# Sparse-attention heads with the scaling ahead of the turns and a transposed output, bias rows by another path, and stage borders in another order

## The chip, the cores and the metric
One core of one Trainium2 chip runs the whole program. The metric is the device time of one execution in microseconds (us), as the median of several runs; less is better.

## The reference
A sequence of 256 tokens, D = 1024, goes through two blocks. The first: short convolution, squared-ReLU mlp, a gated per-layer embedding (ple), dilated window attention with rotary positions (qkv, wo), a second mlp and ple. The second: two layers, each with a half SwiGLU feed-forward, a mixer and a half feed-forward, where the first mixer is an S5 state-space layer and the second is sparse attention over keys and values computed once, between the layers. Everything is f32 in and out; each stage starts with an RMS norm.
```python
def second_block(...):
    for layer in range(DEPTH):                                   # 2
        h = h + 0.5 * _swiglu(_rmsnorm(h, ffn1_norm), w_in, w_out)   # ffn0, ffn2
        u = _rmsnorm(h, mix_norm[layer])
        h = h + (_s5_mixer(u, ...) if layer < 1 else _nsa_mixer(u, kv, ...))
        h = h + 0.5 * _swiglu(_rmsnorm(h, ffn2_norm), w_in, w_out)   # ffn1, ffn3
        if layer == 0:
            kv = _shared_kv(h, ...)        # 6 x 4 heads of 64; 15 compressed blocks

# _nsa_mixer: 16 query heads on 4 kv heads, head_dim 64
o_cmp = softmax(q @ k_cmp * scale + bias_cmp) @ v_cmp            # 256 x 15
o_slc = softmax(q @ k_slc * scale + bias, causal) @ v_slc        # 256 x 256
o_win = softmax(q @ k_win * scale + bias, causal) @ v_win        # 256 x 256
o = gates[..., 0:1] * o_cmp + gates[..., 1:2] * o_slc + gates[..., 2:3] * o_win
return o @ w_o
```
With 256 tokens the selection (8 blocks of 64) and the window (512) both take in the whole sequence. bias is a relative-position table of 32 buckets, so row t of a head's bias is a piece of one vector of distances, shifted by t.

## The kernel before
The activation h stays in SBUF, transposed (channels in partitions). The weights, 280 units of 128 x 2048 f32 (1 MB each), come by SP's queue into a ring of three slots `raw` (L372 to L397): SP issues the next unit when DVE has finished with its slot (`lo_ready`). ACT copies each unit to `w_hi` (L1024), DVE subtracts to get `w_lo` (L1749, `split`), and PE multiplies in split precision (`double_unit` L453 and L455, `exact` L407 to L409). The order of the work on each engine is written out by hand, with semaphores between the engines; nothing is scheduled by a compiler. Zero matmuls (`keep_warm` L510, L513) fill some of PE's pauses.

**A stage border.** A norm is: ACT squares (L1048), POOL adds them (L1545), PE sums over the channels (`norm_sum` L515), DVE takes the variance (L1766), POOL the power (L1553), DVE forms a diagonal (L1770), PE spreads it to all channels (`norm_bcast` L524, L526), ACT copies it to `rs`. DVE's part is `norm(n)` (L1764). In `mlp` (L1831) and `ffn` (L1869) DVE runs it behind `whole(0)` (L1826, a sum of two PSUM banks, recorded at L1828) and `split(g)`. In `ple` (PE L622, DVE L1927) four gate units are multiplied into two banks, so PE waits for DVE's `gate_scaled` ahead of the third and fourth. Behind the first ple DVE computes the rotary angles in eight steps (L2032 to L2040), waits for ACT's sines (`sin_ready`), and only then runs the norm for qkv.

**The tables of S5.** POOL builds eight tables of the state-space kernel in `make_table` (L1611), four of them beside each mlp, in a chain that waits for its own stores; PE takes one at positions `TABLE_AT` (L156) of the mlp's units in `table_turn` (L539, L548) and waits for `tab_ready` (L1634) there.

**The bias rows.** In ffn1 ACT issues, one for each pair of units, `side_loads` (L1134): a store of two heads of the bias vector, each 128 times, to DRAM (L1138, `bias_rows`, 16 x 128 x 383 floats in all), and a load of a piece of `cmp_w1` (L1141). ACT waits for all stores ahead of ffn2, and in ffn2 it loads the rows back (`load_rows` L1144, L1150) into `tbl` with a stride of 382, so that each partition gets its shifted row.

**The heads.** Sixteen heads, one step each (L1008 to L1018 on PE). PE: `n_turn(h)` waits for the exps, turns (transposes) six tiles of 128 x 128 and two of 15 columns (L966, L969) behind 8 zero matmuls (16 for the first); `n_scores(h+1)` (L938) multiplies q with the two key sets and the compressed keys, `n_values(h)` (L972, L985 to L993) multiplies the turned probabilities, stationary, with the values, 64 columns each; every second head `n_turn_out` (L997, L1004) turns the combined output back, behind 6 zero matmuls. ACT: `n_copy` (L1489) copies the first branch and the compressed part out of PSUM, `n_exp` (L1497, L1501 to L1506) takes the exps with their sums, `n_high` (L1510) the high half of the output. DVE: `window_copy` (L2323, L2327) copies the second branch, `logits` (L2303, L2309 to L2320) scales, adds the bias and takes the maxima, `combine` (L2329) forms gate / denominator (L2333, L2336) and scales and sums the three outputs (L2348, L2350), `n_low` (L2353) gives the low half. POOL does nothing in the heads.

## Time and profile before
| | |
|---|---|
| runs shown, median (lowest to highest) | 2113.27 us (2112.58 to 2115.02), 3 runs |
| the profiled execution | 2118.91 us, its span 2116.7 us |
| PE / DVE / ACT / POOL busy | 1976.0 (93%) / 1326.1 (63%) / 934.8 (44%) / 581.7 (27%) us |
| chain that ended last | PE 66%, DVE 12%, ACT 6%, POOL 6%, issue 5%, ACT's queue 3% |
| mean granted clock of PE | 0.967 |
| zero matmuls (L513) in the whole span | 356 recorded in the page's group, 95.1 us |
| weight units | 280 of 1024 KB, 4.8 us from issue to landing (median) |

The profile shows one execution. Busy time of an engine is the time its instructions ran; PE's clock is what the throttle granted, 1.00 being 2.4 GHz and 0.50 being 1.2 GHz. "Idle before, releaser" is how long an engine stood still ahead of an instruction, and what it waited for; "issue" is idle time in which it waited for nothing that the profile shows. The chain that ended last is followed back from the last instruction, at each step to what released it.

### The profile page before, as it was taken

The page shows a single profiled execution, that of the slowest core. Times are in us where ns is not written, and L with a number is a line of the kernel's source. Part 1 is how long each engine was busy: PE and PEld are TensorE (multiplying, and loading weights), DVE is VectorE, ACT ScalarE, POOL GpSimd, SP SyncE. Part 2 cuts the span into 40 slices and gives each one's busy share as a digit, 9 for nine tenths or more (in the row PEclk, how much of TensorE's full clock was granted, in tenths as well). Part 3 has the DMA queues.
Part 4 walks back from the last instruction along what each step waited for, and adds up shares of the span by engine and source line. Part 5 has one row for each costly group of instructions (what it writes and reads, how often), then busy time and mean ns, then how long its engine had stood idle before and what let it go on. Part 6 is the DMA issues. An engine that isn't in the chain of part 4 may idle for free.

```text
span 2116.7 us, 32243 instructions
## 1 busy us (share of the span) xinstructions
PE 1976.0 (93%) x13621; PEld 1779.6 (84%) x13655; DVE 1326.1 (63%) x1653; ACT 934.8 (44%) x1196; POOL 581.7 (27%) x692
## 2 busy tenths in 40 slices
PE   8989998999988998989998999878999989999999
PEld 7979997899987998959997888778799976667998
DVE  6877666566556676666667565456466665546665
ACT  4344454444444444444442353245544453434443
POOL 6967831543223978410005300000000000000000
PEclk9999999999999999999999899999999989999999
DMA  6446663443432455565545156454255520004552
GB/s 240 179 159 219 215 223 123 174 150 140 148 132 112 187 214 194 189 241 187 188 179 184 56 181 227 162 188 160 106 198 196 192 110 21 1 1 159 181 189 108
DMA packets 54939, 339.48 MB, mean 160 GB/s; under 512 B 5995, under 2 KB 13196, under 8 KB 17932
## 3 DMA queue, kind: packets, MB, share of 16 engines
q1 hardware_dynamic: 41552, 295.41, 38.1%
q10 hardware_dynamic: 9276, 27.34, 3.7%
q0 software_dynamic: 3968, 14.68, 2.0%
q8 instruction: 108, 1.77, 0.3%
q14 instruction: 35, 0.29, 0.0%
HBM read 318.54 MB, written 18.87 MB: 159 GB/s over the span
## 4 chain that ended last, share of the span: by engine, by line
PE 66%; DVE 12%; ACT 6%; POOL 6%; issue 5%; ACTq 3%; DMA 1%; POOLq 0%; DVEq 0%
PE psum L453 17%; PE psum L407 10%; PE psum L409 10%; PE psum L408 10%; PE psum L455 9%; DVE w_lo L1749 4%; ACT w_hi L1024 3%; ACTq L1141 2%; PE psum L513 2%; DVE both L1756 1%; POOL pw L1625 1%; ACT both L1024 1%; POOL pw L1624 1%; DVE h L1762 1%; POOL st L1626 1%
## 5 line engine op out<-in xcount | busy, mean ns | idle before, releaser
L1749 DVE TENSOR_TENSOR w_lo<-raw,w_hi 128x2048 fp32r<-128x2048 f32 x277 | 649.7, 2349 | 249.2 <-ACT w_hi L1024 246.3
L453 PE MATMUL psum<-both,w_hi 128*128 128x512 f32 x2112 | 759.3, 402 | 8.1 <-DVE both L1756 4.3
L1024 ACT ACTIVATE w_hi<-raw 128x2048 fp32r<-128x2048 f32 x280 | 533.1, 1907 | 151.1 <-PE psum L409 142.3
L455 PE MATMUL psum<-both,w_lo 128*128 128x256 f32 x2112 | 596.4, 282 | 0.0
L453 PEld LDWEIGHTS psum<-both,w_hi 128*128 128x128 f32 x2112 | 401.2, 190 | 107.2 <-DVE both L1756 6.4
L407 PE MATMUL psum<-both,w_hi 128*128 128x256 f32 x1472 | 432.6, 294 | 37.1 <-DVE w_lo L1749 22.6
L408 PE MATMUL psum<-both,w_hi 128*128 128x256 f32 x1472 | 423.1, 287 | 0.0
L409 PE MATMUL psum<-both,w_lo 128*128 128x256 f32 x1472 | 422.6, 287 | 0.0
L455 PEld LDWEIGHTS psum<-both,w_lo 128*128 128x128 f32 x2112 | 403.3, 191 | 0.3
L407 PEld LDWEIGHTS psum<-both,w_hi 128*128 128x128 f32 x1472 | 288.8, 196 | 37.3 <-DVE w_lo L1749 18.7
L1545 POOL TENSOR_TENSOR ssum<-sq 128x512 f32<-128x512 f32 x13 | 20.2, 1557 | 1016.1 <-ACT sq L1048 956.4
L408 PEld LDWEIGHTS psum<-both,w_hi 128*128 128x128 f32 x1472 | 289.1, 196 | 2.0 <-issue 1.4
L409 PEld LDWEIGHTS psum<-both,w_lo 128*128 128x128 f32 x1472 | 288.5, 196 | 0.0
L1024 ACT ACTIVATE sq<-psum 128x512 f32<-128x512 f32 x120 | 71.5, 596 | 310.5 <-PE psum L455 310.4
L407 PE MATMUL psum<-hid_hi,w_hi 128*128 128x256 f32 x640 | 184.4, 288 | 4.2 <-DVE w_lo L1749 3.3
L408 PE MATMUL psum<-hid_lo,w_hi 128*128 128x256 f32 x640 | 181.9, 284 | 0.0
L409 PE MATMUL psum<-hid_hi,w_lo 128*128 128x256 f32 x640 | 181.8, 284 | 0.0
L407 PEld LDWEIGHTS psum<-hid_hi,w_hi 128*128 128x128 f32 x640 | 123.5, 193 | 8.0 <-DVE w_lo L1749 4.6
L408 PEld LDWEIGHTS psum<-hid_lo,w_hi 128*128 128x128 f32 x640 | 123.5, 193 | 0.1
L409 PEld LDWEIGHTS psum<-hid_hi,w_lo 128*128 128x128 f32 x640 | 123.5, 193 | 0.0
L1828 DVE TENSOR_TENSOR ta<-psum,sq 128x512 f32<-128x512 f32 x76 | 52.3, 688 | 108.9 <-ACT sq L1024 108.9
L513 PE MATMUL psum<-zero 128*128 128x512 bf16 x356 | 95.1, 417 | 12.6 <-DVE both L2355 7.2
(349 smaller groups left out, 2569.4 us busy)
## 6 DMA issues: line engine op xcount, KB each, us to landing
raw<-in_weights SPq DMA_DIRECT2D x280, 1024.0 KB, 4.8
table<-tables ACTq DMA_DIRECT2D x8, 1792.0 KB, 8.5
tables<-st POOLq DMA_DIRECT2D x16, 512.0 KB, 4.6
tables<-st POOLq DMA_DIRECT2D x8, 384.0 KB, 4.4
bias_rows<-bv ACTq DMA_DIRECT2D x8, 383.0 KB
tables<-st POOLq DMA_DIRECT2D x8, 256.0 KB, 7.4
w<-in_cmp_w ACTq DMA_DIRECT2D x4, 512.0 KB, 27.4
tbl<-in_cmp_w ACTq DMA_DIRECT2D x4, 512.0 KB, 30.8
```

The costliest lines, as they stand in the source:

```text
L407: nc.tensor.matmul(out, a_hi, b_hi, start=start, stop=False, skip_group_check=True)
L408: nc.tensor.matmul(out, a_hi, b_lo, start=False, stop=False, skip_group_check=True)
L409: return nc.tensor.matmul(out, a_lo, b_hi, start=False, stop=stop, skip_group_check=True)
L453: nc.tensor.matmul(bank, wh[:, cols], both[x][:, c].rearrange("p e t -> p (e t)"), start=c == 0, stop=False, skip_group_check=True)
L455: return nc.tensor.matmul(bank[:, 0:SEQ], wl[:, cols], x_hi[x][:, c], start=False, stop=c == KC - 1, skip_group_check=True)
L513: nc.tensor.matmul(bank, zero[:, 0:P], zero[:], start=True, stop=True, skip_group_check=True)
L1024: copy = lambda out, in_, **kw: nc.scalar.activation(out, in_, ACT.Copy, **kw)
L1141: act.dma_start([w1[:], w1v][k // 4][:, at], A["cmp_w1"][k // 4][:, at])\
L1624: tt(pw[:, 0], old, a_re, ALU.mult)
L1625: link(tt(pw[:, 1], old, a_im, ALU.mult))
L1749: tt(w_lo[:, g % RING], raw[:, g % RING], w_hi[:, g % RING].bitcast(F32), ALU.subtract).then_inc(sem["lo_ready"], 1)
L1828: tt(ta[:], hi_part(pair), low[into], ALU.add).then_inc(sem["a_sum"], 1)
```

## The change
**Heads.** The softmax factor (gate / denominator) is now multiplied into the probabilities ahead of the turns: the first branch on DVE (`scale`), the second branch and the compressed part on POOL. The values are now the stationary side and the turned probabilities the moving one, all three branches are summed in one PSUM region of 64 x 256, already transposed, so the combine and the turn of the output go. The logits of both branches are written by wide operations over two neighbouring banks. ACT makes all copies. All zero matmuls in the heads go. PE's order in a step is values of two heads back, scores of the next, turn of the last.
**Bias rows.** One store of the bias vector (16 x 383); 128 row loads of one partition each on SP, four behind each of 32 weight loads from ffn2's fourth unit on.
**Borders.** DVE's norm goes ahead of `whole(0)` and `split(g)` in `mlp` and `ffn`; ple's gate units go to four places in three banks; the rotary angles go into the first ple's loop and the norm ahead of the wait for the sines; three of the table positions of the second mlp move by one.
```diff
-TABLE_AT = ((1, 4, 8, 12), (2, 6, 10, 14))
+TABLE_AT = ((1, 4, 8, 12), (3, 7, 11, 14))
...
+    bias_v = A["bias_v"].tensor
+    def bias_row(p):
+        row = bass.AP(bias_v, P - 1 - p, [[NH * NDIST, 1], [NDIST, NH], [1, SEQ]])
+        sp.dma_start(tbl[p:p + 1], row).then_inc(sem["tbl_landed"], 16)
...
             sp.wait_ge(sem["lo_ready"], RING * k + (u + 1 - RING))
             sp.dma_start(raw[:, u:u + 1], A["weights"][bass.ds(RING * k + u, 1)]
                          .rearrange("o p n -> p o n")).then_inc(raw_landed[u], 16)
+            at = RING * k + u - BASE["ffn2"] - RING
+            if at == 0:
+                sp.wait_ge(sem["bias_stored"], 16)
+                sp.wait_ge(sem["hid_done"], 4)
+            if 0 <= at < 32:
+                for p in range(4 * at, 4 * at + 4):
+                    bias_row(p)
...
+    GB = [DB[3], U[0], U[1], DB[3]]
...
         for m in range(PAIRS):
-            if m >= 2:
-                pe.wait_ge(sem["gate_scaled"], PAIRS * l + m - 1)
-            up_unit(g + 1 + m, 0, XBUF[n], U[m % 2], (sem["xl_ready"], XBASE[n], 1) if m == 0 else None,
+            if m == 3:
+                pe.wait_ge(sem["gate_scaled"], PAIRS * l + 1)
+            up_unit(g + 1 + m, 0, XBUF[n], GB[m], (sem["xl_ready"], XBASE[n], 1) if m == 0 else None,
                     (lambda: norm_sum(n)) if m == 0 else (lambda: norm_bcast(n)) if m == 1 else None)
         pe.wait_ge(sem["gate_scaled"], PAIRS * (l + 1) - 1)
...
         for br in range(2):
-            bank = DB[2 * br + b]
+            bank = DB[2 * b + br]
...
     def n_turn(hd):
         b = hd % 2
-        if hd >= 2:
-            pe.wait_ge(sem["n_lo"], hd // 2)
         if hd:
-            pe.wait_ge(sem["n_tv"], hd)
             pe.wait_ge(sem["n_ta"], hd)
-        keep_warm(8 if hd else 16, U[0])
-        pe.wait_ge(sem["n_exp"], hd + 1)
+        pe.wait_ge(sem["n_near"], hd + 1)
+        pe.wait_ge(sem["n_far"], hd + 1)
         for br in range(2):
             for j in range(3):
-                last = nc.tensor.transpose(U[br][:, j * P:(j + 1) * P], lg[:, b, br, j * P:(j + 1) * P],
-                                           ident)
-        for t in range(TT):
-            last = nc.tensor.transpose(MB[0:NCMP, t * P:(t + 1) * P], lgc[:, b, t, :], ident)
+                nc.tensor.transpose(U[br][:, j * P:(j + 1) * P], lg[:, b, br, j * P:(j + 1) * P], ident)
+            last = nc.tensor.transpose(U[br][0:NCMP, 3 * P:4 * P], lgc[:, b, br, :], ident)
         last.then_inc(sem["n_t"], 1)
     def n_values(hd):
-        b, kh = hd % 2, 2 * (hd // 8) + hd % 2
-        if hd:
-            pe.wait_ge(sem["n_part"], 3 * hd)
-        pe.wait_ge(sem["n_tv"], hd + 1)
+        b, kh, ch = hd % 2, 2 * (hd // 8) + hd % 2, hd // 2
+        out = [XB, MB][ch % 2][b * HD:(b + 1) * HD, 0:SEQ]
+        if b == 0 and ch >= 2:
+            pe.wait_ge(sem["n_lo"], ch - 1)
         pe.wait_ge(sem["n_ta"], hd + 1)
         dims = slice(kh * HD, (kh + 1) * HD)
-        def out(br, t):
-            at = (br * TT + t) * HD
-            return XB[:, at:at + HD]
-        for t in range(TT):
-            nc.tensor.matmul(out(0, t), ptc[:, b, t * P:(t + 1) * P], vcmp[:, kh, :], start=True, stop=True,
+        nc.tensor.matmul(out, vcmp[:, kh, :], ptc[:, b, :], start=True, stop=False, skip_group_check=True)
+        for br in range(2):
+            nc.tensor.matmul(out, vs[:, br, 0, dims], ptn[:, b, br, 0:SEQ], start=False, stop=False,
                              skip_group_check=True)
-        for br in range(2):
-            pb_ = ptn[:, b, br]
-            nc.tensor.matmul(out(1 + br, 0), pb_[:, 0:P], vs[:, br, 0, dims], start=True, stop=True,
-                             skip_group_check=True)
-            nc.tensor.matmul(out(1 + br, 1), pb_[:, P:2 * P], vs[:, br, 0, dims], start=True, stop=False,
-                             skip_group_check=True)
-            last = nc.tensor.matmul(out(1 + br, 1), pb_[:, 2 * P:3 * P], vs[:, br, 1, dims], start=False,
-                                    stop=True, skip_group_check=True)
+            last = nc.tensor.matmul(out[:, P:SEQ], vs[:, br, 1, dims], ptn[:, b, br, SEQ:SEQ + P], start=False,
+                                    stop=br == 1, skip_group_check=True)
         last.then_inc(sem["n_pv"], 1)
-    def n_turn_out(ch):
-        keep_warm(6, U[0])
-        pe.wait_ge(sem["n_part"], 6 * ch + 6)
-        if ch:
-            pe.wait_ge(sem["n_lo"], ch)
-        for t in range(TT):
-            last = nc.tensor.transpose(MB[:, SEQ + t * P:SEQ + (t + 1) * P],
-                                       oc[:, ch % 2, t].rearrange("p e d -> p (e d)"), ident)
-        last.then_inc(sem["n_ot"], 1)
     n_scores(0)
-    for step in range(NH + 1):
-        if step:
-            n_turn(step - 1)
+    for step in range(NH + 2):
+        if step >= 2:
+            n_values(step - 2)
         if step + 1 < NH:
             n_scores(step + 1)
-        if step:
-            n_values(step - 1)
-        if step and step % 2 == 0:
-            n_turn_out(step // 2 - 1)
+        if 1 <= step <= NH:
+            n_turn(step - 1)
     residual_units("nwo", 0, (sem["n_lo"], 0, 2))
...
         act.wait_ge(sem["bv_copied"], 1)
+        act.dma_start(A["bias_v"], bv[:]).then_inc(sem["bias_stored"], 16)
     def side_loads(k):
         if 0 <= k < PIECES:
-            heads = slice(NH // PIECES * k, NH // PIECES * (k + 1))
-            act.dma_start(A["bias_rows"][heads], bv[heads].unsqueeze(1)
-                          .broadcast_to([NH // PIECES, P, NDIST])).then_inc(sem["bias_stored"], 16)
             at = slice(CL // 4 * (k % 4), CL // 4 * (k % 4 + 1))
             act.dma_start([w1[:], w1v][k // 4][:, at], A["cmp_w1"][k // 4][:, at])\
                 .then_inc(sem["cmpw_landed"], 16)
-    def load_rows(k):
-        if k < PIECES:
-            at = NH // PIECES * k
-            rows_ = bass.AP(A["bias_rows"].tensor, P - 1 + at * P * NDIST,
-                            [[NDIST - 1, P], [P * NDIST, NH // PIECES], [1, SEQ]])
-            act.dma_start(tbl[:, at:at + NH // PIECES], rows_).then_inc(sem["tbl_landed"], 16)
...
-            if f == 2:
-                load_rows(k)
...
-    act.wait_ge(sem["bias_stored"], 16 * PIECES)
...
-        copy(ptn[:, b, 0], U[0][:, 0:3 * P])
-        copy(ptc[:, b], MB[0:NCMP, 0:SEQ]).then_inc(sem["n_ta"], 1)
+        for br in range(2):
+            copy(ptn[:, b, br], U[br][:, 0:3 * P])
+            last = copy(ptc[:, b, br * P:(br + 1) * P], U[br][0:NCMP, 3 * P:4 * P])
+        last.then_inc(sem["n_ta"], 1)
...
+    for hd in range(NH):
+        b = hd % 2
+        pool.wait_ge(sem["n_fac"], hd + 1)
+        for t in range(TT):
+            pool.tensor_scalar(lgc[:, b, t], lgc[:, b, t], fac[:, b, 0, t:t + 1], None, ALU.mult)
+        pool.tensor_scalar(lg[:, b, 1, 0:P], lg[:, b, 1, 0:P], fac[:, b, 2, 0:1], None, ALU.mult)
+        pool.tensor_scalar(lg[:, b, 1, P:3 * P], lg[:, b, 1, P:3 * P], fac[:, b, 2, 1:2], None,
+                           ALU.mult).then_inc(sem["n_far"], 1)
...
         split(late)
+        norm(n)
         whole(0, hb)
         split(g)
-        norm(n)
         dve.wait_ge(sem["rs_ready"], n + 1)
...
         if late is not None:
             split(late)
+        if n is not None:
+            norm(n)
         whole(0, hb)
         split(g)
         if n is not None:
-            norm(n)
             dve.wait_ge(sem["rs_ready"], n + 1)
...
+    def angles(m):
...
-            tt(ta[:], two(U[m % 2]), rs_b, ALU.mult).then_inc(sem["gate_scaled"], 1)
+            tt(ta[:], two([DB[3], U[0], U[1], DB[3]][m]), rs_b, ALU.mult).then_inc(sem["gate_scaled"], 1)
             gated(PAIRS * l + m + 1, two([XB, DB[0], DB[1], DB[2]][m]), m)
             if x:
                 x_low(r, m)
             if m < 2:
                 split(g + 1 + m)
+            if l == 0:
+                angles(m)
...
+    norm(R_PLE0)
     dve.wait_ge(sem["sin_ready"], 3)
-    norm(R_PLE0)
...
-        stt(lgc[:, b].rearrange("p t c -> p (t c)"), DB[b][:, 3 * P:3 * P + TT * NCMP], NSCALE,
+        stt(lgc[:, b].rearrange("p t c -> p (t c)"), DB[2 * b][:, 3 * P:3 * P + TT * NCMP], NSCALE,
             cmp_bias[:, :, hd], ALU.mult, ALU.add)
-        for br in range(2):
-            bank = DB[2 * br + b]
-            stt(lg[:, b, br, 0:P], bank[:, 0:P], NSCALE, near, ALU.mult, ALU.add)
-            last = stt(lg[:, b, br, P:3 * P], bank[:, P:3 * P], NSCALE, far, ALU.mult, ALU.add)
-        last.then_inc(sem["n_log"], 1)
+        banks = psum[:, 2 * b:2 * b + 2]
+        stt(lg[:, b, :, 0:P], banks[:, :, 0:P], NSCALE, near.unsqueeze(1).broadcast_to([P, 2, P]),
+            ALU.mult, ALU.add)
+        stt(lg[:, b, :, P:3 * P], banks[:, :, P:3 * P], NSCALE, far.unsqueeze(1).broadcast_to([P, 2, SEQ]),
+            ALU.mult, ALU.add).then_inc(sem["n_log"], 1)
         dve.wait_ge(sem["n_log"], hd + 1)
         dve.tensor_reduce(nm[:, b, 0, :], lgc[:, b], AX.X, ALU.max, negate=True)
-        for br in range(2):
-            dve.tensor_reduce(nm[:, b, 1 + br, 0:1], lg[:, b, br, 0:P], AX.X, ALU.max, negate=True)
-            last = dve.tensor_reduce(nm[:, b, 1 + br, 1:2], lg[:, b, br, P:3 * P], AX.X, ALU.max, negate=True)
-        last.then_inc(sem["n_max"], 1)
-    def window_copy(hd):
-        dve.wait_ge(sem["n_t"], hd + 1)
-        if hd >= 2:
-            dve.wait_ge(sem["n_pv"], hd - 1)
-        dve.tensor_copy(ptn[:, hd % 2, 1], U[1][:, 0:3 * P]).then_inc(sem["n_tv"], 1)
-    def combine(hd):
+        dve.tensor_reduce(nmx[:, b], lg[:, b].rearrange("p r (j k) -> p r j k", j=3), AX.X, ALU.max,
+                          negate=True).then_inc(sem["n_top"], 1)
+        dve.wait_ge(sem["n_top"], hd + 1)
+        tt(nm[:, b, 1:3, 1], nmx[:, b, :, 1], nmx[:, b, :, 2], ALU.min).then_inc(sem["n_max"], 1)
+    def scale(hd):
         b = hd % 2
         dve.wait_ge(sem["n_exp"], hd + 1)
@@ -2335,35 +2324,24 @@
         dve.wait_ge(sem["n_rec"], hd + 1)
         tt(fac[:, b], fac[:, b], gate[:].rearrange("p t (r n) -> p r t n", n=NH)[:, :, :, hd],
            ALU.mult).then_inc(sem["n_fac"], 1)
-        dve.wait_ge(sem["n_pv"], hd + 1)
         dve.wait_ge(sem["n_fac"], hd + 1)
-        for br in range(3):
-            if br:
-                dve.wait_ge(sem["n_part"], 3 * hd + br)
-            for t in range(TT):
-                at = (br * TT + t) * HD
-                out = oc[:, hd // 2 % 2, t, b]
-                f = fac[:, b, br, t:t + 1]
-                if br:
-                    last = stt(out, XB[:, at:at + HD], f, out, ALU.mult, ALU.add)
-                else:
-                    last = ts(out, XB[:, at:at + HD], f, None, ALU.mult)
-            last.then_inc(sem["n_part"], 1)
+        ts(lg[:, b, 0, 0:P], lg[:, b, 0, 0:P], fac[:, b, 1, 0:1], None, ALU.mult)
+        ts(lg[:, b, 0, P:3 * P], lg[:, b, 0, P:3 * P], fac[:, b, 1, 1:2], None,
+           ALU.mult).then_inc(sem["n_near"], 1)
     def n_low(ch):
         dve.wait_ge(sem["n_hi"], ch + 1)
-        tt(x_lo[0][:, ch], MB[:, SEQ:2 * SEQ], x_hi[0][:, ch].bitcast(F32),
+        tt(x_lo[0][:, ch], [XB, MB][ch % 2][:, 0:SEQ], x_hi[0][:, ch].bitcast(F32),
            ALU.subtract).then_inc(sem["n_lo"], 1)
-    for step in range(NH + 1):
-        if step:
-            window_copy(step - 1)
+    for step in range(NH + 2):
         if step < NH:
             logits(step)
-        if step:
-            combine(step - 1)
-        if step and step % 2 == 0:
-            n_low(step // 2 - 1)
+        if 1 <= step <= NH:
+            scale(step - 1)
+        if step >= 5 and step % 2:
+            n_low((step - 5) // 2)
+    n_low(NQ - 1)
     residual_stage("nwo", R_NWO)
     ffn(3, R_NWO, R_FFN3, x=False, late=BASE["nwo"] + 3)
```

## Rows read from the trace of the kernel before
**Rows 1.** Busy time by stretch: PE, PEld, DVE, ACT, POOL, PE clock, DMA share, GB/s
```profile
1755.85:1894.45 138.60, 126.14 (x763) 91.65 (x777) 77.36 (x311) 53.64 (x231) 0.00 (x0) 0.95 0.00 1
1234.01:1449.15 215.14, 189.82 (x1208) 172.83 (x1209) 120.00 (x106) 85.95 (x85) 4.06 (x3) 0.94 0.55 186
1522.51:1705.76 183.25, 180.92 (x1205) 165.24 (x1206) 120.92 (x106) 87.45 (x86) 4.04 (x3) 1.00 0.52 191
130.30:137.10 6.80, 5.23 (x15) 4.44 (x16) 3.32 (x5) 1.92 (x4) 6.34 (x10) 0.50 0.61 248
935.80:939.20 3.40, 3.40 (x12) 2.90 (x11) 0.69 (x1) 2.57 (x4) 0.00 (x0) 0.50 0.98 418
```
**Rows 2.** Groups of instructions in the heads (busy, mean ns, idle before)
```profile
L513 PE MATMUL psum<-zero 128*128 128x512 bf16 x170 | 45.5, 408 | 8.2 <-DVE both L2355 7.2 <-issue 0.6
```
**Rows 3.** Timeline of PE in one head (start, duration, line)
```profile
1812.98 0.82 PE L966 MATMUL psum<-con,lg 128*128 128x128 f32 x6
...
1813.94 0.48 PE L944 MATMUL psum<-ks,q 64*128 64x128 f32 x2
...
1814.27 0.59 PE L946 MATMUL psum<-ks,q 64*128 64x256 f32 x2
...
1814.70 0.38 PE L944 MATMUL psum<-ks,q 64*128 64x128 f32 x2
...
1815.80 0.65 PE L985 MATMUL psum<-vcmp,ptc 15*128 15x64 f32 x4
```
**Rows 4.** Timeline of ACT in the same head
```profile
1814.05 0.49 ACT L1024 ACTIVATE ptn<-psum 128x384 f32<-128x384 f32 x1 [3.33 <-PE psum L969]
...
1814.44 0.36 ACT L1024 ACTIVATE ptc<-psum 15x256 f32<-15x256 f32 x1
```
**Rows 5.** Timeline of DVE in the same head
```profile
1814.53 0.19 DVE L2309 SCALAR_TENSOR_TENSOR lgc<-psum,cmp_bias 128x30 f32<-128x30 f32 x1
...
1816.95 0.18 DVE L2333 RECIPROCAL fac<-dn 128x6 f32<-128x6 f32 x1
```
**Rows 6.** POOL's scalings, lines L1647 and L1581 (duration min/median/max)
```profile
L1647 POOL TENSOR_SCALAR st<-st x8: 858/863/1063, 103.5 to 858.4; 128x256 f32<-128x256 f32 x8
...
L1581 POOL TENSOR_SCALAR sm<-a x1: 312/312/312, 29.9 to 29.9; 128x32 f32<-128x32 f32 x1
```
**Rows 7.** Timeline of PE: norm_bcast at mlp0, qkv, ffn0 and ffn3
```profile
131.87 1.22 PE L526 MATMUL psum<-diag,ones 128*128 128x256 f32 x2 [3.56 <-DVE diag L1770]
...
375.66 1.22 PE L526 MATMUL psum<-diag,ones 128*128 128x256 f32 x2 [6.19 <-DVE diag L1770]
...
935.20 0.70 PE L526 MATMUL psum<-diag,ones 128*128 128x256 f32 x2 [2.58 <-DVE diag L1770]
...
1931.13 0.70 PE L526 MATMUL psum<-diag,ones 128*128 128x256 f32 x2 [3.34 <-DVE diag L1770]
```
**Rows 8.** Timeline of DVE: the angles, and ffn3's start
```profile
368.36 0.29 DVE L2033 CAST ang<-posi 128x256 f32<-128x256 int32 x1
...
371.11 0.29 DVE L2040 TENSOR_SCALAR ang<-ang 128x256 f32<-128x256 f32 x1
...
1926.76 0.68 DVE L1828 TENSOR_TENSOR ta<-psum,sq 128x512 f32<-128x512 f32 x1
...
1929.69 0.15 DVE L1766 TENSOR_SCALAR var_tok<-psum 128x2 f32<-128x2 f32 x1
```
**Rows 9.** Timeline of PE and POOL: table turns and the fourth table in mlp1
```profile
799.72 1.54 PE L548 MATMUL psum<-con,ab 128*128 128x128 f32 x6 [6.16 <-POOL st L1634]
...
845.25 0.20 POOL L1634 COPY st<-e 128x8 f32<-128x8 f32 x1
...
848.25 1.04 PE L548 MATMUL psum<-con,ab 128*128 128x128 f32 x8
```
**Rows 10.** DMA issues on ACT and SP by line (time held, min/median/max)
```profile
L1141 ACTq DMA_DIRECT2D tbl<-in_cmp_w x4: 6352/15442/19212, 1338.0 to 1399.3; - x4
...
L388 SPq DMA_DIRECT2D raw<-in_weights x276: 327/328/328, 18.1 to 2077.9; - x138
```

60 lines of the change are left out of this document (32 added, 28 removed).

## The prediction

> **What bounds the kernel now.** I read the engines' shares first: PE is busy 93% of the span and carries 66% of the chain that ended last, so time goes only where PE idles, runs zero products, or runs at the lower clock. The table by stretch [rows 1] shows where that is. In the heads PE is "busy" 126.1 of 138.6 us, but 45.5 us of that are zero matmuls [rows 2]; POOL does nothing there, DVE and ACT are busy about half. ffn1 needs 215.1 us for its body, ffn2 183.3 for the same products, with PE busy 189.8 and 180.9: that is a stall. The last two stretches show PE at half clock (0.50, the 1.2 GHz level) behind a pause at a stage border. Then I read, engine by engine, one step of the heads [rows 3 to 5] and the borders [rows 7 to 9]. The sum is made against the profiled execution, 2118.9 us; the median of the runs shown is 5.6 lower, which I take off at the end. A measurement of this kernel can tell about 0.2% (4.2 us).
>
> **Heads.** Before, 138.6 / 16 = 8.66 us a head: one chain (turn, copies, products, combine) whose gaps the zero matmuls fill. The 184 zero matmuls go, yet what they cover is waiting, so their 45.5 us are not the gain; the new period is. PE's loop is now turn(h), a wait for its copies, values(h), scores(h+3), turn(h+1). In one head [rows 3]: turn 1812.98 to 1813.94 = 0.96; scores 1813.94 to 1815.80 = 1.86; a product over 256 columns 0.43 (1814.27 to 1814.70), so new values, three of 256 and two of 128 columns, 3x0.43 + 2x0.22 = 1.73. ACT now copies both banks: 2x0.39 (starts 1814.05 and 1814.44) plus two 15-partition pieces, bounded by 0.36 for 256 columns [rows 4], taken 0.2 each, plus drain: 1.27. PE's loop if nothing else bounds: 0.96 + 0.1 + 1.27 + 0.1 + 1.73 + 1.86 = **6.0**.
> The other loop goes through DVE and POOL. DVE's logits(h+2) wait for turn(h) and stand in its queue ahead of the factor of h+1; POOL's scaling of h+1 waits for that factor, and turn(h+1) for the scaling; the exps lie beside it. Serial: turn 0.96 + 0.1; logits and maxima, 1814.53 to 1816.95 = 2.42 (now wider but the same columns; the reduces cover 768 at once); reciprocal 0.18 [rows 5] and a product of its size, 0.39 with what lies between; POOL's scalings of 15, 15, 128 and 256 columns. No row shows POOL scaling with a per-partition pointer. The nearest are 0.86 for 128x256 and 0.31 for 128x32 [rows 6], so 0.27, 0.27, 0.55, 0.86 = 1.95, taken 2.2 with a little for each pointer; bounds 1.8 and 3.2. With it, 0.96 + 0.1 + 2.42 + 0.39 + 2.2 + 0.1 = **6.2** a head. ACT's share, 53.6 / 16 = 3.35 [rows 1] plus the copy taken over, and DVE's, 77.4 / 16 = 4.8 less the combine, stay under it. So POOL's loop just binds: 10.7 until the pipeline is full, 15 x 6.2, 3.1 behind the last: about 106. With the zeros gone PE is idle some 4 us ahead of the first turn and some 2 us a head later; I add 3 for the start and 5 for stretches at half clock (before, even with zeros, 0.95 [rows 1]). 114 against 138.6: **-25**, between -33 (POOL 1.8, no clock loss) and -18 (POOL at 2.7, 6.7 a head: 8 us more).
> POOL and DVE now both scale at the same time. No row shows such a pair. The Trainium skill, "SBUF — State Buffer", "Who interferes with whom", says that a tensor_scalar in DVE's two-port mode and a GpSimd operation lock each other out wholly; by it each head would lose up to 0.5, DVE's two scalings at no more than the 0.29 of a scaling of 256 columns [rows 8], and the total would come out near 2042.
>
> **Bias rows, the ACT queue in ffn1.** Eight stores of two heads x 128 copies x 383 floats become one of 16 x 383. Before, the eight loads of cmp_w1 queued behind these stores held ACT, the last four 6.4 to 19.2 us each [rows 10], so its copies of the weights, and PE with them, came late. With short queues ffn1 should run as ffn2 does: 215.14 - 183.25 = **-31.9** [rows 1]. Ends: 0 (the loads of cmp_w1 hold ACT by themselves) to -32. I take the whole: the hold grows from piece to piece (loads of equal size, 6.4 at the least, 19.2 at the most), as it would behind stores that pile up, and not if it were the load's own cost.
> **Row loads on SP.** 128 small DMAs, four behind each of 32 weight loads. An issue on SP takes 0.33 us [rows 10], so four take 1.3 of the 5.7 us that a unit lasts (183.25 over some 32 units); the DMA share in ffn2 is 0.52 [rows 1], and 128 rows of 16 KB put 2 MB beside its 32. The wait on the bias store lies far behind it, and the wait on the compressed hidden states is met before ffn2's first split. ACT loses eight issues. **0**, hidden by the slack of a ring of three; bounds -1 and the rival below.
>
> **Norm ahead of whole and split.** At each border PE waits for DVE's diag [rows 7]: 3.56 (mlp0), 2.58 (ffn0), 3.34 (ffn3). In ffn3 DVE does whole and split from 1926.76 to 1929.69 first [rows 8]: 2.9 us that now follow the norm. What is late next is the first relu or SwiGLU product, which needs the broadcast anyway, and the split of the next unit, 2 units ahead. mlp0: wait 3.56 to about 0.3, -3.2; behind it PE runs at half clock with 5.23 busy in 6.8 [rows 1], full clock would save 2.6: **-5.8**. ffn0: -2.6 and half of the 3.4 at 0.50 [rows 1]: **-4.3**. ffn3 likewise: **-4.4**. ffn1's small wait is left at 0. The clock part is the choice here; without it the three give 6 us less.
> **qkv's start.** PE waits 6.19 for diag [rows 7]; DVE does the angles from 368.36 to 371.40, 3.0 us [rows 8], then waits for ACT's sines until the norm. The norm no longer waits for them: -3.3 and a part of the clock. But six of the eight steps, 2.3 of the 3.0, now lie ahead of ple0's last x_low, which the same norm needs; the rope waits later then end sooner. **-4** of a possible -6.
> **mlp1 and the tables.** The norm saves 3 here too, but POOL's tables bound this stage: PE waits 6.16 for one at 799.72, and the fourth is ready only at 845.25, turned at 848.25 [rows 9]. POOL starts 2.9 earlier, so the fourth is there at about 842.3. Positions 3, 7, 11 for 2, 6, 10 put the turns later where they waited; the fourth position is unchanged, so PE arrives there early and the stall goes to the last table. End of the stage: 848.25 to 842.3, -5.9, less 2.4 of half clock behind a wait of some 10 us: **-3.5**.
> **ple.** Gates in other banks take two PE waits away, but DVE's and ACT's gate work sets that stage: **0** (bounds -2, +1).
> Sum: 25 + 31.9 + 5.8 + 4.3 + 4.4 + 4 + 3.5 = 78.9. 2118.9 - 78.9 = 2040.0; less 5.6: **2034**.
>
> **Rivals.**
> (a) PE's clock. The zeros held the clock; without them PE idles 2 of 6.2 us a head, and if the chip grants 1.2 GHz throughout, PE's part 4.55 doubles: 10.7 a head, 174 us for the heads, 60 more: 2094. For: the half-clock stretches [rows 1] follow pauses of 3 us. Against: a pause here is 2 us or less, and turns recur. 0.12, mostly in milder forms of 2040 to 2075.
> (b) POOL at 1.8 and no clock loss: PE's loop binds, 6.0 a head, about 2023. 0.17.
> (c) The change does not do what it says in ffn1: the hold is cmp_w1's own, 512 KB a load with pieces of its own; none of the last four was issued in less than 6.4 us [rows 10]. Then 31.9 stays: 2066. 0.12.
> (d) Slower. The row loads do on SP what the stores did on ACT. A store had 256 pieces (2 heads x 128) and held the issue behind it up to 19.2 us [rows 10], 0.075 a piece. Four rows are 64 pieces, 4.8 us a unit, in series with a weight load's 4.8 (the profile's section of DMA issues): 9.6 against 5.7 a unit, 3.9 x 32 = 125 more: 2159. It decides from 79 / 32 = 2.5 us a unit, or 0.053 a piece: 3.4 us a unit, of which 5.7 - 4.8 = 0.9 is slack. Against: the 0.52 share of DMA in ffn2 leaves room. 0.05.
> The store's access pattern has an outermost dimension of 2 heads, a row load's of 16. By the Trainium skill, "DMA: Bandwidth & Descriptors", "Why a DMA increments its semaphore by 16 and not by 1", the engines used are the largest number up to 16 that divides that dimension: two for the store, 16 for a row. By that rule the long hold of 19.2 us is the store's and (c) and (d) both fall away.
> **How the numbers follow.** Forecast 0.54, (a) 0.12, (b) 0.17, (c) 0.12, (d) 0.05. The range goes from (b) with a little more (2014) to beyond (c) (2074); it leaves out (d), the full form of (a) and a sum with two misses. Faster in all but (d) and the worst of (a) with (c): 0.93; within 0.2%: 0.01; slower: 0.06.
>
> **What would show it.** Heads: 6.0 to 6.4 us between turns, POOL busy about 2.2 a head, n_turn waiting for POOL rather than ACT; granted clock 0.9 or more. ffn1's body 183, no ACT issue over 3 us. ffn2's body 183 still. Diag waits under 1 us. In mlp1 one long wait at the fourth table near 832. Wrong if the heads' clock reads 0.5, if ffn1 stays above 200, or if ffn2 grows.

## The result, and the profile after

The changed kernel takes 2083.35 us (median of 4 runs, 2074.79 to 2089.9) where the kernel before takes 2114.14; the ratio is 0.985, interval 0.9803 to 0.9896. It is 1.5% faster, by 31 us where 79 were forecast, and lies outside the range of 2014 to 2074. Its runs are 15 us apart, those of before 5. One execution of one experiment (e9), the profiled one, took 2330.6 us at a mean clock of 0.746; its time and its trace are left out below. The profiled execution took 2088.89 us, 30.0 less than the one of before.

The page of the changed kernel: engines, PE's clock in 40 slices, and the chain that ended last.
```profile
PE 1966.1 (94%) x13339; PEld 1768.8 (85%) x13359; DVE 1301.9 (62%) x1509; ACT 941.0 (45%) x1228; POOL 619.9 (30%) x756
...
PEclk9999999999999999999998999999999975569999
...
PE 69%; DVE 11%; POOL 9%; ACT 7%; issue 3%; DMA 1%; ACTq 0%; POOLq 0%; DVEq 0%
```
Four slices stand out at 7, 5, 5 and 6 tenths: they are the heads. ACT's queue, 3% of the chain before, is gone from it.

The table by stretch of the changed kernel, which answers to [rows 1]: the heads, the bodies of ffn1 and ffn2, and the end of mlp1 from the fourth table's turn to the next broadcast.
```profile
core 0: us, PE busy (x) PEld busy (x) DVE busy (x) ACT busy (x) POOL busy (x), PEclk, DMA share, GB/s
1707.40:1868.70 161.30, 137.97 (x480) 96.42 (x480) 54.11 (x170) 59.52 (x263) 35.68 (x64) 0.55 0.00 1
1218.97:1402.70 183.73, 181.40 (x1207) 165.82 (x1208) 121.02 (x106) 86.93 (x85) 4.04 (x3) 1.00 0.54 201
1474.60:1658.19 183.59, 181.27 (x1206) 165.66 (x1206) 121.01 (x106) 87.49 (x86) 4.04 (x3) 1.00 0.55 190
834.01:874.78 40.77, 38.85 (x296) 38.33 (x298) 23.44 (x37) 14.98 (x19) 17.03 (x37) 0.88 0.46 168
```
The heads grew from 138.6 to 161.3 us, with the clock at 0.55 for 0.95. PE has 480 records there for 763, yet was busy 138.0 us for 126.1. ffn1's body fell from 215.14 to 183.73, just ffn2's. The last stretch took 36.47 us before, at full clock:
```profile
848.25:884.72 36.47, 34.54 (x298) 34.02 (x298) 28.02 (x40) 17.79 (x22) 19.11 (x35) 1.00 0.68 243
```

One step of the heads on PE, timeline of the changed kernel (start, duration), with the pause between turn and values:
```profile
1780.30 0.90 PE L978 MATMUL psum<-con,lg 128*128 128x128 f32 x3
...
1783.61 1.08 PE L990 MATMUL psum<-ptc,vcmp 15*64 15x256 f32 x2 [1.34 <-ACT ptc L1012]
...
1787.37 0.79 PE L959 MATMUL psum<-ks,q 64*128 64x128 f32 x2
...
1790.90 0.90 PE L978 MATMUL psum<-con,lg 128*128 128x128 f32 x3
```
A step is 1780.30 to 1790.90 = 10.6 us: turn and copies 3.3, values and the issue behind them 3.8, scores 3.5. These are the terms of the forecast with each of PE's about doubled; the copies alone kept their 1.3. Of the fifteen steps between turns nine take 10.5 to 10.6 us at a clock of 0.50, four 9.5 to 9.7 at 0.56 to 0.62, and the last two 7.3 and 4.9. The waits of PE in the heads say what bounds:
```profile
PE psum L990 <- ACT ptc L1012: 20.6, 16, 1.3
PE psum L978 <- POOL lg L1715: 2.7, 2, 2.5
```
PE waits 16 times for the copies and only twice for POOL. POOL's scalings, of which no row was at hand, came as estimated, 1795.78 to 1798.00 = 2.22 us for 2.2 (x2 stands for two instructions merged in one line):
```profile
1795.78 0.75 POOL L1713 TENSOR_SCALAR lgc<-lgc,fac 128x15 f32<-128x15 f32 x2 [8.37 <-DVE fac L2325]
...
1796.50 0.60 POOL L1714 TENSOR_SCALAR lg<-lg,fac 128x128 f32<-128x128 f32 x1
...
1797.08 0.92 POOL L1715 TENSOR_SCALAR lg<-lg,fac 128x256 f32<-128x256 f32 x1
```

The borders, which answer to [rows 7]: the broadcasts of mlp0, qkv and ffn3 on PE.
```profile
128.71 0.70 PE L541 MATMUL psum<-diag,ones 128*128 128x256 f32 x2 [0.67 <-DVE diag L1755]
...
366.48 0.70 PE L541 MATMUL psum<-diag,ones 128*128 128x256 f32 x2 [0.38 <-DVE diag L1755]
...
1902.69 0.70 PE L541 MATMUL psum<-diag,ones 128*128 128x256 f32 x2 [0.43 <-DVE diag L1755]
```
Waits of 3.56, 6.19 and 3.34 became 0.67, 0.38 and 0.43. DMA issues that touch `tbl`, which answer to [rows 10] (ns held, min/median/max):
```profile
L388 SPq DMA_DIRECT2D tbl<-bias_v x128: 481/589/2236, 1457.8 to 1633.8; - x128
...
L1127 ACTq DMA_DIRECT2D tbl<-in_cmp_w x4: 334/334/335, 1314.2 to 1365.4; - x4
```
The loads of cmp_w1 that held ACT for 6.4 to 19.2 us hold it for 0.33. A row load costs SP 0.59.

From broadcast to broadcast (the stages' first broadcasts in both traces), forecast against measured, in us:

| stage | forecast | measured |
|---|---|---|
| mlp0 and ple0 | -5.8 | -7.1 |
| qkv, with its part of the clock in attention | -4 | -4.1 (40.87 to 38.78, and 298.32 to 293.31 less mlp1's earlier norm, 3.0) |
| mlp1 | -3.5 | +1.3 (3.0 earlier, then 210.74 to 215.00) |
| ffn0 | -4.3 | -4.4 (19.73 to 16.98, 190.92 to 189.24) |
| ffn1 with its start | -31.9 | -32.1 |
| kv, ffn2, qg | 0 | -1.1 |
| heads | -25 | +22.6 (138.7 to 161.3) |
| nwo, ffn3 | -4.4 | -4.9 |

Two rows failed: the heads by 47.6 and mlp1 by 4.8. All others together were forecast within 4 us.

### The profile page after: what moved, and what is told of

Read it like the earlier page. It is cut to its first block, busy times and chain, and to the rows that moved or that the text cites. A ratio compares the mean times of both kernels' runs of the same rounds, so it can differ in the third digit from the quotient of the medians.

```text
span 2086.8 us, 31686 instructions
## 1 busy us (share of the span) xinstructions
PE 1966.1 (94%) x13339; PEld 1768.8 (85%) x13359; DVE 1301.9 (62%) x1509; ACT 941.0 (45%) x1228; POOL 619.9 (30%) x756
## 4 chain that ended last, share of the span: by engine, by line
PE 69%; DVE 11%; POOL 9%; ACT 7%; issue 3%; DMA 1%; ACTq 0%; POOLq 0%; DVEq 0%
PE psum L468 19%; PE psum L421 10%; PE psum L423 10%; PE psum L422 10%; PE psum L470 10%; DVE w_lo L1734 4%; ACT w_hi L1012 3%; DVE both L1741 2%; POOL pw L1602 1%; PE psum L992 1%; POOL pw L1601 1%; PE psum L961 1%; PE psum L978 1%; POOL st L1603 1%; ACT both L1012 1%
## 5 line engine op out<-in xcount | busy, mean ns | idle before, releaser
L1662 POOL TENSOR_TENSOR swap<-swap,sin_rs 32x512 f32<-32x512 f32 x24 | 44.6, 1859 | 122.7 <-DVE swap L2082 122.7
```

The source lines that it names most:

```text
L1662: pool.tensor_tensor(swap[:], swap[:], sin_rs[0:32].unsqueeze(1).broadcast_to([32, 2, SEQ]), ALU.mult).then_inc(sem["sin_part"], 1)
```

## The experiments

Times are medians, with the ratio to the kernel before, run on the same chip beside it. Those kernels before took 2114 to 2117 us, so between two experiments the ratios compare better than the times. "Heads" is the time from the first scores to the last values, "step" the time between two turns. Five theories meet in the heads: the clock fell in the pause ahead of the first turn; the pause between turn and values keeps it down; the share of time in which PE is busy does; the kind of work (turns, products on 64 rows) does; or the clock only follows, and a new loop of turn, copies and values bounds the step (the "dependency theory").

**e1, the heads of before in the changed kernel.** Edit: PE, ACT, DVE and POOL heads put back, of which on PE:
```diff
-                pe.wait_ge(sem["n_near"], hd + 1)
-                pe.wait_ge(sem["n_far"], hd + 1)
+                keep_warm(8 if hd else 16, U[0])
+                pe.wait_ge(sem["n_exp"], hd + 1)
...
+                if step and step % 2 == 0:
+                    n_turn_out(step // 2 - 1)
```


> The changed kernel with the heads of before (their zero matmuls and combine too); all else of the change stays. Between before and after the stages other than the heads lose 52.5 us by the traces and the heads gain 22.6. If the parts add up: heads 138.7 us, time 2114 - 52.5 = 2061 to 2062, and it beats the changed kernel by some 20. If a part of the gain elsewhere came only together with the new heads, it is above 2065.

Measured 2068.8 us, ratio 0.9783 (0.976 to 0.9806), heads 138.3. The rest of the change is worth 48 us by the kernel before beside it (2116.5) for the 52.5 of the sum; the new heads cost 14 of it by the medians. The time lies above the 2065 that was to mean that a part of the gain came only with the new heads. The trace doesn't bear that out: ahead of the heads it is 3.2 us behind the changed kernel's, mainly 1.6 by the first broadcast, 1.6 in mlp0 (200.6 for 199.0) and 1.3 in ffn2's stretch, and the first two differences stand also between kernels that have the same code there (in mlp0 e2 took 200.4, e5 199.1).

**e2, scores ahead of values.**
```diff
-                if step >= 2:
-                    n_values(step - 2)
                 if step + 1 < NH:
                     n_scores(step + 1)
+                if step >= 2:
+                    n_values(step - 2)
```


> In a step PE's scores go ahead of the values, so that ACT's copies of a turn run beside the scores and not in an idle PE (1.3 us a head). Clock theory (PE's idle time lets the clock fall, and at 1.2 GHz PE's own work sets the step of 10.6): the step is PE's work alone at half clock, 10.6 - 1.3 - 0.5 = 8.8 to 9, heads 145 or less (less where the busier engine gets full clock at times), time 2060 to 2068. Dependency theory (the new loop turn, copies, values bounds, and the clock only follows): the step falls to 6.2 to 7 at once, time below 2040. Kind-of-work theory (turns and products of 64 rows do not hold the clock however dense they are): granted clock stays 0.5, heads 145, 2068.

Measured 2046.6 us (2045.0 to 2049.2), ratio 0.9674 (0.9652 to 0.9695), heads 114.9. The first step took 9.2 at half clock; then the clock rose and stayed for eleven steps. Behind them it fell twice more, for 6.8 us each time, and came back (steps of 7.4, 7.0 and 6.2). One full step and a stretch of eight, timeline and table by stretch of e2:
```profile
1758.81 0.52 PE L978 MATMUL psum<-con,lg 128*128 128x128 f32 x3 [1.43 <-POOL lg L1715]
...
1759.80 0.48 PE L959 MATMUL psum<-ks,q 64*128 64x128 f32 x2
...
1761.66 0.64 PE L990 MATMUL psum<-ptc,vcmp 15*64 15x256 f32 x2
...
1765.17 0.52 PE L978 MATMUL psum<-con,lg 128*128 128x128 f32 x3 [1.43 <-POOL lg L1715]
```
```profile
1745.00:1796.00 51.00, 39.46 (x240) 29.21 (x240) 26.73 (x84) 30.07 (x134) 18.04 (x34) 1.00 0.00 1
```
The step is 6.36 us and PE waits for POOL ahead of the turn, both as forecast (6.2). The theory of the kind of work falls: the same turns and products run at 1.00. No total of the three was met: the step is that of the dependency theory (6.2 to 7), the 2046.6 is not (below 2040).

**e3, eight zero matmuls of 256 columns in the pause.**
```diff
+                for _ in range(8):
+                    nc.tensor.matmul([XB, MB][ch % 2][:, SEQ:2 * SEQ], zero[:, 0:P], zero[:, 0:SEQ],
+                                     start=True, stop=True, skip_group_check=True)
                 pe.wait_ge(sem["n_ta"], hd + 1)
```


> Eight zero matmuls of 256 columns (0.85 us at full clock) in the pause between a turn and the values, into unused columns of the output's bank. Clock theory by idle share: PE is busy 5.4 of 6.2 us again, as dense as before the change (126 of 138.6), granted clock 0.9 or more, step 6.2 to 6.5, heads 105 to 115, time 2030 to 2042. Dependency theory or kind-of-work theory: at half clock the zeros take 1.7 us where 1.3 were idle, step 11, time about 2090.

Measured 2042.8 us, ratio 0.9656 (0.9636 to 0.9677), heads 108.3, step 6.36 in the changed kernel's own order:
```profile
1737.40:1800.00 62.60, 57.87 (x375) 43.59 (x376) 33.43 (x105) 36.72 (x162) 21.53 (x40) 1.00 0.01 1
```
Putting 128 zero matmuls of half the width back gains 40 us over the changed kernel. The dependency theory falls here, since the order is unchanged and the step is 6.36, not 11. Heads met what was expected, the total misses it by 1.

**e4, scores first and 8 wide zero matmuls ahead of each turn** (`keep_warm(8 if hd else 16, U[0])` behind the wait on `n_ta`).

> Scores ahead of the values, and 8 zero matmuls of 512 columns (1.7 us at full clock) ahead of each turn's wait for the scalings, 16 ahead of the first. Clock theory: PE is busy nearly always, clock 0.95 or more, step max(6.2, 4.55 + 1.7 + 0.2) = 6.45, heads 103 to 112, time 2028 to 2040. If the clock stays at 0.5 whatever fills the pauses: step 9 + 3.4 = 12.4, heads 200, time 2120.

Measured 2043.0 us, ratio 0.9659 (0.9637 to 0.9681), clock 1.00 from the first turn on, step 6.58: the zeros just overrun the wait they fill. Heads 112.0, at the upper end of what was expected; the total misses it by 3.

**e5, a full clock at the start only** (`keep_warm(28, U[0])` for head 0, none later).

> 28 zero matmuls ahead of the first turn alone, none later: the heads begin at full clock. Start theory (the clock fell in the pause ahead of the first turn, and the step at half clock, with its pause between turn and values, never earns it back): it stays near 1.0, step 6.4 as in the two kernels with full clock, heads 108 to 116, time 2040 to 2048. Pause theory (the step of the changed kernel loses the clock by itself, wherever it begins): it falls within a few steps, step 9.5 to 10.6, heads 150 to 165, time 2078 to 2090.

Measured 2077.8 us (2071.2 to 2088.7), ratio 0.9825 (0.9785 to 0.9866). The table by stretch of e5, five steps before and five after the fall:
```profile
1731.10:1762.80 31.70, 24.95 (x151) 18.22 (x151) 16.52 (x52) 18.56 (x82) 11.14 (x20) 1.00 0.00 1
1772.50:1825.30 52.80, 46.35 (x152) 32.26 (x151) 16.87 (x53) 18.55 (x82) 11.14 (x20) 0.50 0.00 1
```
The same work takes 31.7 us and then 52.8. The start theory falls: the order runs at full clock for six steps of 6.35 and loses it in the seventh. It then stays at half clock for 68 us, till the last steps, though PE is busy 88% there and 79% before. That is the pause theory's course, but later than "within a few steps": heads 143.6 in this trace, for 150 to 165. The runs' times go with their mean clocks (0.962 at 2071.2, 0.950 at 2088.7; in the changed kernel 0.956 at 2074.8, 0.947 at 2089.9), so the spread is probably how long the heads stay at half clock; only one execution of each was profiled, so this is not shown.

**e6, e3's zeros on 64 rows** (`zero[0:64, 0:P], zero[0:64, 0:SEQ]`).

> The eight zero matmuls of 256 columns in the pause, but over 64 rows of the array instead of 128. If all columns count alike: as with 128 rows, step 6.36, 2039 to 2045. If rows count: half clock, step 11, 2090.

Measured 2045.9 us (2 runs), ratio 0.9669 (0.9644 to 0.9695), heads 118.6, 10 more than e3: two steps at half clock (11.0 and 10.0), then 6.36. Once the clock is up, 64 rows hold it. The return was slow: PE ran the first 19.8 us behind the first turn at half clock without a pause, where e3 ran 3.0.
```profile
1719.65:1739.44 19.79, 19.79 (x68) 12.98 (x69) 6.35 (x20) 7.22 (x32) 4.47 (x8) 0.50 0.00 1
```
Whether that is the rows or chance, one trace doesn't tell.

**e7, turns in the pause** (eight `nc.tensor.transpose(..., ident, ident)` for e3's zeros).

> Eight f32 transposes of the identity (128 columns each, 0.9 us at full clock) in the same pause instead of zero matmuls. If turns keep the clock as products do: step 6.4, 2040 to 2046. If turns do not count: the clock stays 0.5 and they add 1.9 us where 1.3 were idle, step 11.2, time 2090 to 2100.

Measured 2037.0 us (2 runs), ratio 0.9627 (0.9601 to 0.9654), heads 112.5, full clock from the second step on. The Trainium skill, "TensorE: Matmul & The Clock Gate", "Part 4: PE-mode transpose", says that turns don't count as PE being busy in the same way. Here f32 turns in the pause held the clock at 1.00 as well as zero matmuls did; in this trace the rule doesn't decide.

**e8, the loop shortened.** e2, 3 zero matmuls ahead of each turn, and the far branch's 256 columns scaled by DVE:
```diff
-                pool.tensor_scalar(lg[:, b, 1, P:3 * P], lg[:, b, 1, P:3 * P], fac[:, b, 2, 1:2], None,
-                                   ALU.mult).then_inc(sem["n_far"], 1)
...
+                ts(lg[:, b, 1, P:3 * P], lg[:, b, 1, P:3 * P], fac[:, b, 2, 1:2], None,
+                   ALU.mult).then_inc(sem["n_near"], 1)
```


> Scores ahead of values, 3 zero matmuls of 512 columns ahead of each turn (16 ahead of the first), and the 256-column scaling of the far branch moved from POOL to DVE. If the loop turn, logits, factor, scaling bounds the step at full clock as the forecast says, it loses POOL's 0.92 and becomes 5.4 to 5.5, heads 96 to 99, time 2024 to 2030. If DVE's three scalings and POOL's two hold each other up, POOL's 128 columns take over 0.6 each and the step stays at 5.9 or more, 2034.

Measured 2030.9 us, ratio 0.96 (0.9581 to 0.9618), step 5.50 as expected; heads 100.4 and the time lie about 1 above what was expected. Timeline of e8, POOL and DVE, and twelve steps in its table by stretch:
```profile
1761.16 0.86 POOL L1714 TENSOR_SCALAR lgc<-lgc,fac 128x15 f32<-128x15 f32 x2 [4.18 <-DVE fac L2325]
...
1761.59 0.39 DVE L2330 TENSOR_SCALAR lg<-lg,fac 128x256 f32<-128x256 f32 x1
...
1761.87 0.60 POOL L1715 TENSOR_SCALAR lg<-lg,fac 128x128 f32<-128x128 f32 x1
```
```profile
1729.70:1795.70 66.00, 65.05 (x392) 47.12 (x398) 43.45 (x137) 44.89 (x200) 15.79 (x36) 1.00 0.00 1
```
The step lost 0.86 of POOL's 0.92, so the loop of the forecast did bound it, as PE's wait of 1.43 for POOL in e2 says too. Now PE is busy 65.05 of 66.00 us and waits for no engine: its own work with the three zero matmuls bounds. POOL's first two scalings grew from 0.75 to 0.86 beside a third one of DVE, the 0.60 did not grow. Of the 0.5 a head that the rule of the Trainium skill, "SBUF — State Buffer", "Who interferes with whom" (named in the prediction), put at risk, 0.1 shows in this step; in the changed kernel the first scaling of 15 columns, beside DVE's two, took 0.56 and the second 0.34, so that some 0.1 may be lost there already (an estimate from these two).

**e9, the old table positions on e8.**

> On the fastest kernel so far (e8: scores ahead of values, three zero matmuls, far branch's 256 columns on DVE), the table positions of before, 2, 6, 10, 14 for 3, 7, 11, 14. Theory: POOL's chain sets mlp1, and the later positions only gathered PE's waits into one of 11.5 us at the fourth table, behind which PE runs 4.3 us longer than before the change; with the old positions the wait is split over the third and fourth, the stage from broadcast to broadcast falls from 214.95 to 211 to 212, time 2027 to 2028. Rival: the later positions are what keeps the stage at 215, then the old ones give 217 or more and 2033.

Measured 2032.3 us (3 runs, 2030.6 to 2034.0), ratio 0.9599 (0.9581 to 0.9617), where e8 has 0.96. The 3 to 4 us less of the theory do not show. The total is within 1 of the rival's 2033, but its 2 us over e8 are less than the interval, and no trace shows the stage: by the times alone the positions are worth nothing that can be told.

**e10, the old bias path on e8** (stores and row loads on ACT back, SP's out).

> e8 with the bias rows by the old path (eight stores and eight loads on ACT, no row loads on SP). If the whole 31.9 us of ffn1 are the stores': ffn1 to kv 224.6 for 193.3, time 2030.9 + 31.5 = 2062. If cmp_w1's loads held ACT in part: less than 31 more. If the row loads on SP cost anything in ffn2, ffn2's stretch falls by it.

Measured 2053.0 us, ratio 0.9697 (0.9681 to 0.9712), 22 more than e8. ffn1's body in e8 and in e10:
```profile
1221.15:1405.07 183.92, 181.60 (x1207) 165.79 (x1208) 121.03 (x106) 86.97 (x85) 4.04 (x3) 1.00 0.56 200
```
```profile
1215.89:1427.03 211.14, 192.08 (x1209) 174.94 (x1208) 120.05 (x106) 86.02 (x85) 4.04 (x3) 0.94 0.57 190
```
The path costs 27.2 us in its stage, 4 less than expected, and the total is 9 below the 2062 that was expected. The issues of the eight loads of cmp_w1 held ACT for 92.2 us together in e10, 95.4 in the kernel before and 2.7 in the changed one: the hold comes with the stores, and it was 3 us shorter here. ffn2's stretch is 255.3 for 255.5, so that the row loads on SP cost nothing that can be seen. The total moved 5 less than the stage; in the two traces the S5 mixer, between ffn0 and ffn1, was 2.4 shorter in e10, and other stages by less.

**e11, DVE's norm behind whole and split again, on e8.**

> e8 with DVE's norm behind whole and split again in both mlps and all ffns. Forecast: mlp0 +5.8, ffn0 +4.3, ffn1 +1, ffn3 +4.2, time some 14 to 15 more but for mlp1. In mlp1 theory A (a split that runs beside POOL's table chain holds POOL up by about 2 us each; with the norm first two more splits fall into it) gives POOL the chain of before, 172.7 from its power to the fourth table for 175.4 to 178, so that mlp1 ends no later than now: total 2043 to 2045. Theory B (the chain's length is chance, and the norm first is a gain there too): mlp1 3 more, 2047 to 2049, chain 175 or more.

Measured 2042.0 us, ratio 0.9639 (0.962 to 0.966), 11 more than e8. By stages mlp0 +3.2, ffn0 +2.8 and +1.6, ffn3 +4.3, attention and mlp1 together +4.6, and, where nothing was edited, the S5 mixer -3.8 and the heads -5.2, which happened to begin at full clock. POOL's chain to the fourth table took 178.1, not 172.7: theory A's number is missed. Its first part shows: the first table came 28.6 us behind POOL's power with four splits in that time, 31.0 with five. The rest can't be told from chance: with one and the same code in this stage the chain took from 175.4 (the changed kernel, e8) to 178.1 us (e2).

**e12 and e14, zero matmuls in the wait for the fourth table.** e12 on e8; e14 takes 60 and, ahead of the first turn of the heads, 8 for 16:
```diff
+                if c == 7:
+                    keep_warm(44, MB)
                 pe.wait_ge(sem["tab_ready"], c + 1)
```


> e8 with 44 zero matmuls of 512 columns (9.4 us at full clock) in PE's wait of 11.5 us for the fourth table of mlp1. If what the stage lost behind that wait is the clock (40.8 us from the fourth turn to the next broadcast for 36.5 before the change): 4 us less, stage 211, time 2026 to 2027. If it is something else: 2031 as before, or 1 to 3 more where the zeros are late.

> e12 with 60 zero matmuls for 44 in the wait for the fourth table, and 8 for 16 ahead of the first turn of the heads (where 16 at half clock take 6.8 us and delay it). If the clock behind the fourth table is what the stage lost and e12's zeros were only too few for its wait (3.8 us stayed idle): 36.5 us from the turn to the next broadcast for 40.5, stage 212 to 214; heads up to 4 less; time 2020 to 2026. If neither: 2031.

Measured: e12 2025.75 us (2019.1 to 2032.4), ratio 0.9568 (0.9539 to 0.9597); e14 2025.6 (2023.9 to 2026.8), ratio 0.9583 (0.9554 to 0.9613). From the fourth turn to the next broadcast, e12 and e14:
```profile
837.84:878.30 40.46, 38.56 (x298) 37.94 (x298) 23.62 (x37) 15.01 (x19) 17.10 (x37) 0.89 0.46 170
```
```profile
835.60:872.07 36.47, 34.55 (x297) 34.02 (x297) 24.68 (x37) 14.99 (x19) 16.74 (x36) 1.00 0.52 188
```
In e12 the fourth table came later, 3.8 us stayed idle behind the zeros, and nothing was won in this stretch; that its total met the expectation is due to heads of 95.2 us, which happened to begin at full clock. In e14 the wait was filled: clock 1.00 and 36.47, to the hundredth what it was before the change. What mlp1 lost behind its long wait is the clock. The fewer zeros at the heads' start brought nothing (heads 100.0 for 100.4).

**e13, more work with the pause left as it is** (the changed order, 8 wide zero matmuls ahead of each turn).

> The changed kernel's order with 8 zero matmuls of 512 columns (1.7 us at full clock) ahead of each turn's wait, 16 ahead of the first; the pause of 1.3 us between a turn and its values stays as it is. Share theory (what counts is the share of time in which PE works): at full clock PE would be busy 4.6 + 1.7 of 7.7 us a step, 81%, more than the 72% of e2, which kept the clock; then full clock, step 7.6 to 7.8, heads 130 to 138, time 2056 to 2066. Pause theory (the pause between turn and values, which a lower clock doesn't shorten, keeps the clock from coming back once it is lost): half clock for most of the heads, step up to 13.7, heads 170 to 215, time 2095 or more.

Measured 2063.9 us, ratio 0.9766 (0.973 to 0.9802), heads 131.1, as the share theory expected (its step was to be 0.1 shorter):
```profile
1736.60:1800.00 63.40, 52.47 (x302) 35.47 (x305) 26.71 (x84) 29.90 (x132) 17.83 (x32) 1.00 0.00 1
```
Clock 1.00, step 7.93, PE busy 83%, and the pause of 1.3 us is still there: the pause alone does not bring the clock down. That it keeps a lost clock from coming back is not tested by e13, whose clock was up before the first turn and never fell. The share alone does not decide the fall either: at 77% (39.46 of 51.00) e2 lost the clock after eleven steps, at 79% (24.95 of 31.70) e5 after six. The two differ in the return. Table by stretch at half clock, of the changed kernel, then of e2:
```profile
1741.22:1799.25 58.03, 51.48 (x164) 35.43 (x165) 19.00 (x61) 21.31 (x96) 13.38 (x24) 0.50 0.00 0
```
```profile
1724.00:1733.58 9.58, 9.58 (x32) 6.81 (x33) 3.17 (x10) 3.61 (x16) 2.24 (x4) 0.50 0.00 0
```
```profile
1805.26:1812.09 6.83, 6.83 (x25) 4.67 (x24) 2.39 (x8) 3.02 (x15) 2.24 (x4) 0.50 0.00 0
```
With a pause of 1.3 us in each step PE stood at half clock for 58 us at a time (68 in e5); without one, busy for the whole stretch, the clock was back within 10 us in e2, within 9 in e7 and within 20 in e6 (e2's last fall, with one pause in it, lasted 6.8 too). So the traces agree with the pause theory for the return, but no run changes the pause alone at half clock; the changed kernel's clock did rise twice for 3.4 us in spite of it; and what makes it fall stays open.

## Why the prediction was wrong

- **The term that failed is the clock in the heads.** The forecast took 5 us for "stretches at half clock" from the 0.95 of before. With the clock held the heads take 108.3 us (e3), in the changed kernel 161.3 at 0.55: the term measured 53. The forecast gave the full form a small part of rival (a)'s 0.12, because "a pause here is 2 us or less". Rival (a) was the outcome: its price, PE's 4.55 doubled and 10.7 a head, was met (10.6), and its 2094 is within 11 us of the measured time (its heads of 174 are 13 too long, since the clock rose at times); only its chance was too low. The argument against it was wrong twice: pauses of 1.3 us did not let the clock stay (e5), and the 0.95 of before was the clock with the zero matmuls in it, which the change takes away. An operation whose only purpose is to be work for PE can't be costed at the idle time it fills.
- **The other terms of the heads were right.** At full clock the step is 6.36 (e2, e3) for 6.2, POOL's scalings 2.22 for 2.2, and the loop through POOL bounds (PE's wait in e2, e8), so that rival (b) falls too. With the clock held, e2 and e3 give 2047 and 2043, by 9 to 13 over the forecast of 2034, of which mlp1's miss is 5.
- **Fall and return are not alike.** The changed order ran six steps at the fast pace and then five whole ones at the slow one in e5, and nearly all at the slow one in the profiled run. The forecast asked only whether the clock would fall, not whether it would come back.
- **mlp1, -3.5 forecast, +1.3 measured.** The step that failed is "the fourth is there at about 842.3". POOL began 3.0 earlier and its chain took 175.4 us for 172.7, so that 2.7 of the 3.0 were given back and the table came 0.3 earlier for the 2.9 of the forecast. Part of this goes with DVE's splits (31.0 for 26.3 to the first table, in every trace with the norm first); the rest stays open, as the same code's chains differ by 2.8. The stall did go to the last table, 11.5 us; half clock behind it cost 4.3 (e14) for the 2.4 forecast. The wait, timeline of PE in the changed kernel:
```profile
834.01 1.33 PE L563 MATMUL psum<-con,ab 128*128 128x128 f32 x5 [11.49 <-POOL st L1611]
```
- **The bias rows were right**: 31.4 in the body for 31.9; rival (c) falls with the issues of 0.33 us. e10, which puts the old path back, finds 27 of them. Rival (d) falls: SP pays 0.59 us a row, 2.4 us a unit, and ffn2's body is 183.6.
- **The borders were right** in the size of the waits and of the clock behind them: -4.4 for -4.3 in ffn0, -4.9 for -4.4 at the end, -4.1 for -4 at qkv. The order of the norm alone is worth 12 in mlp0, ffn0 and ffn3 (e11: 3.2, 4.4, 4.3).
- **The best kernels** are e12 and e14, 2026 us, 4.2 to 4.3% under the kernel before and 2.8% under the changed one.

## What to carry to other kernels

Before zero matmuls are taken out, ask what clock the remaining work would be granted, and look at the step as it would be at half clock: if its waits are as long there, it may stay at half clock. Then fill the pauses instead of the whole step, or order the work so that PE's own products lie beside the copies: the order alone gave 37 us here. Where PE must wait for another engine for long, zero matmuls up to the end of the wait pay (4 us for one wait of 11.5, e14), and zeros that end 3.8 us early do not (e12).
